# State scan of a hybrid diffusion block: clamped differences as relu on ScalarE, two multiplies on GpSimd

## The chip, the cores and the metric

One core of a Trainium2 chip runs the whole two-layer program in one launch. The metric is the device time of that launch in microseconds (us); lower is better. The engines are TensorE (PE; its weight loads are PEld), VectorE (DVE), ScalarE (ACT), GpSimd (POOL) and SyncE (SP).

## The reference

Two layers over 1024 latent and 256 context tokens. The second has a long convolution beside a bidirectional state-space scan. The change touches that scan alone, which per direction computes, for chunks of 128 tokens:

```python
acs = jnp.cumsum(adt, axis=-1)
decay_states = jnp.exp(acs[..., -1:] - acs)
states = jnp.einsum('bclgn,bgecl,bclgep->bcgepn', bc, decay_states, x)
...
wdiag = jnp.einsum('bclgn,bcsgn->bgcls', cc, bc)[:, :, None] * jnp.exp(segsum(adt))
y_diag = jnp.einsum('bgecls,bcsgep->bclgep', wdiag, x)
y_off = jnp.einsum('bclgn,bcgepn,bgecl->bclgep', cc, states[:, :-1], jnp.exp(acs))
```

There are 8 heads of 64 columns in 2 groups, state size 128, everything in fp32. segsum takes the differences of the running sums on the lower triangle. Context chunks come first and only carry the state on; latent chunks also give an output y.

## The kernel before, in words

`scan_states` works through 20 units (direction, chunk), the two directions in turn: `units`, of which u = 0 to 3 are context and give no output, and u = 4 to 19 are latent, with output number i = 0 to 15 (the dictionary `Y`). Each engine has its own program over the same units, in the order written, tied by semaphores.

Of one unit:

- GpSimd multiplies a triangle by the rates adt into adt_spread, [128, 8 heads, 128] (L1655, one unit ahead), and x by dt into x_dt (L1664, output units).
- TensorE makes the running sums of all heads along the free axis by a product of adt_spread with all ones (L1587, PSUM banks 0 and 1), and along the partitions by the triangle (L1588, bank 2). It makes them for unit u + 1 right after the state product of unit u (L1605), and ahead of the output products of unit u (L1619 with segments and x_dt, L1620 with the old state and exp_acs). The gram of an output unit (L1598) stands at its start, ahead of its state product.
- ScalarE copies the small sums to acs_source (L1633), takes the exponential of each head's total to decay_chunk (L1634) and, in output units, of all sums to exp_acs (L1639). It then takes the exponential of acs_left to decay_source (L1644) and that of the segments (L1647).
- VectorE takes total less sum to acs_left (L1684, reads PSUM), the differences of all sums to segments (L1689, reads PSUM, 1024 columns), multiplies decay_source by dt (L1691) and x by it to x_weighted (L1696), clamps the segments at zero (L1700), multiplies exp_acs by C (L1705), masks the gram (L1708), multiplies the segments by it (L1712), multiplies the old state by decay_chunk to state_kept (L1718), adds the state product (L1723), and reads the output of the unit before (L1569, or L1572 where it adds to the other direction's).

The state product needs x_weighted; the next running sums wait until all readers of the PSUM banks 0 to 2 are done (act_read, last_made, seg_made). Most tiles have two buffers; state_kept has one.

```python
HL = [P, H, CH]      # 128 x 8 x 128
HX = [P, H, HD]      # 128 x 8 x 64
acs_ps = g.ps[:, 0:2, :].rearrange("p b (h l) -> p (b h) l", l=CH)
by_head = lambda ap, shape: ap.unsqueeze(2).to_broadcast(shape)
```

Of the kernel before, what the change touches and what calls it, by code (L numbers as in the profile page):

```python
# [23 lines left out]
P = 128  # L24
# [1469 lines left out]
def scan_states(nc, g, d, xbc, gate, dt, adt, out):  # L1494
# [44 lines left out]
    names = ("spread sums acs_out act_read last_made seg_made decay_done clamped seg_exp decay_dt weighted x_dt c_scaled gram "  # L1539
             "masked attended state_product kept state y_product y_out cleared")  # L1540
    with stage(nc, names) as (mem, sems):
        (spread, sums, acs_out, act_read, last_made, seg_made, decay_done, clamped, seg_exp, decay_dt, weighted, x_dt,
# [14 lines left out]
        tmp = tile(nc, mem, "state_kept", [P, H, HD])  # L1557
# [4 lines left out]
        with nc.Block() as block:  # L1562
# [12 lines left out]
            def _(pe):  # L1575
                def running_sums(u):
# [3 lines left out]
                    if u >= 1:  # L1580

                        pe.wait_ge(act_read, u)
                        pe.wait_ge(last_made, u)
                        if ny(u):
                            pe.wait_ge(seg_made, ny(u))
# [38 lines left out]
            def _(act):  # L1624
                for u, (dr, c) in enumerate(units):
                    end = CH - 1 if dr == 0 else 0
                    act.wait_ge(sums, u + 1)
                    if u >= 2:
                        act.wait_ge(last_made, u - 1)
                        if ny(u - 1):  # L1630
                            act.wait_ge(seg_made, ny(u - 1))
                        act.wait_ge(kept, u - 1)
                    act.activation(acs[:, u % 2, :], g.ps[:, 2, 0:H], ACT.Copy).then_inc(acs_out, 1)  # L1633
                    done = act.activation(whole[:, u % 2, :], acs_ps[:, :, end], ACT.Exp)  # L1634
                    if u in Y:
                        i = Y[u]
                        if i >= 2:
                            act.wait_ge(y_product, i - 1)
                        done = act.activation(ea[:, i % 2], acs_ps, ACT.Exp)  # L1639
# [5 lines left out]
                    if u in Y:  # L1645
                        act.wait_ge(clamped, i + 1)
                        act.activation(seg[:, i % 2], seg[:, i % 2], ACT.Exp).then_inc(seg_exp, 1)  # L1647

            @block.gpsimd
            def _(pool):  # L1650
# [14 lines left out]

                spread_adt(0)
                for u, (dr, c) in enumerate(units):
                    if u + 1 < U:
                        spread_adt(u + 1)
                    if u in Y:  # L1670
# [3 lines left out]
            def _(dve):  # L1674
                dve.memset(st[:], 0.0).then_inc(cleared, 1)
                dve.wait_ge(cleared, 1)
                for u, (dr, c) in enumerate(units):
                    end = CH - 1 if dr == 0 else 0
                    tok = slice(c * CH, (c + 1) * CH)
                    dve.wait_ge(acs_out, u + 1)  # L1680
                    dve.wait_ge(act_read, u + 1)
                    if u >= 2:
                        dve.wait_ge(decay_done, u - 1)
                    dve.tensor_tensor(last[:, u % 2, :], acs_ps[:, :, end], acs[:, u % 2, :], ALU.subtract).then_inc(last_made, 1)  # L1684
                    if u in Y:
                        i = Y[u]
                        if i >= 2:
                            dve.wait_ge(y_product, i - 1)
                        dve.tensor_tensor(seg[:, i % 2], acs_ps, by_head(acs[:, u % 2, :], HL), ALU.subtract).then_inc(seg_made, 1)  # L1689
# [922 lines left out]
```

## Time and profile before

| what | value |
|---|---|
| median of 3 runs | 4232.28 us (4231.64 to 4232.49) |
| the profiled execution | 4226.73 us, span of its trace 4224.9 us |
| busy share of the span | PE 87%, PEld 64%, DVE 42%, ACT 30%, POOL 3% |
| instructions | 44523 |
| the scan (second stage of `scan_states`) | about 2636 to 2816 us of the span |

The span begins at the first instruction of the trace. Times in the rows below are microseconds from the start of the span unless marked ns; a busy share is over the whole program, of which the scan is about 4%. In a timeline a line gives start, length, engine, source line and operation, output<-inputs with their shape, the count of merged instructions, and in brackets the idle time ahead of it with what ended it. "psum" as the output of a matmul line is followed by its two operands. A length on DVE or POOL includes the time in which the engine was held up inside the instruction.

### The profile page before, as it was taken

The numbers are of one execution on the slowest core, as the hardware profiler recorded it, in microseconds if no ns is written. First come the engines' busy times: TensorE is split into PE (matmuls) and PEld (weight loads), VectorE is DVE, ScalarE is ACT, GpSimd is POOL, SyncE is SP. The second block draws the span as 40 slices with busy tenths as digits, with TensorE's granted clock in tenths as the row PEclk, the third lists the DMA queues.
The fourth block names the chain that finished last, engine by engine and source line by source line (L and its number), as shares of the span: only waits on it lengthen the run. The fifth ranks groups of instructions, "written<-read, shape, count | busy, mean of one in ns | idle before, by whom it ended". The sixth has DMA issues, their size and how long they took to land. (4 is left out here: it accounts for less than half of the span.)

```text
span 4224.9 us, 44523 instructions
## 1 busy us (share of the span) xinstructions
PE 3667.2 (87%) x17492; PEld 2713.8 (64%) x17492; DVE 1786.6 (42%) x2458; ACT 1258.7 (30%) x2138; POOL 134.6 (3%) x108
## 2 busy tenths in 40 slices
PE   6987788788895999999995999756898759999997
PEld 3663466566673888888883877432344538888885
DVE  2222556555407333333336432775255244333334
ACT  3322467666524111111114222220100232221122
POOL 0000000000001000000001000310000010000001
PEclk7998899999997999999998999875999979999998
DMA  7623310110003111111103210001320121111112
GB/s 292 252 93 101 92 26 14 50 35 17 25 17 124 40 36 38 40 37 37 40 25 119 90 50 22 1 34 60 123 84 25 60 94 51 46 49 50 50 45 94
DMA packets 98569, 272.31 MB, mean 64 GB/s; under 512 B 18205, under 2 KB 33053, under 8 KB 94276
## 3 DMA queue, kind: packets, MB, share of 16 engines
q1 hardware_dynamic: 98436, 270.51, 18.9%
q8 instruction: 86, 1.41, 0.1%
q14 instruction: 47, 0.39, 0.0%
HBM read 220.41 MB, written 50.07 MB: 64 GB/s over the span
## 5 line engine op out<-in xcount | busy, mean ns | idle before, releaser
L569 PE MATMUL psum<-h_high,w_high 128*128 128x512 f32 (+1 forms) x1280 | 472.7, 369 | 51.3 <-DVE w_low L648 51.3
L569 PE MATMUL psum<-h_low,w_high 128*128 128x512 f32 (+1 forms) x1280 | 472.3, 369 | 0.0
L569 PE MATMUL psum<-h_high,w_low 128*128 128x512 f32 (+1 forms) x1280 | 471.8, 369 | 0.0
L582 PE MATMUL psum<-hid_low,w_high 128*128 128x512 f32 (+1 forms) x1280 | 471.5, 368 | 0.0
L582 PE MATMUL psum<-hid_high,w_high 128*128 128x512 f32 (+1 forms) x1280 | 471.3, 368 | 0.0
L582 PE MATMUL psum<-hid_high,w_low 128*128 128x512 f32 (+1 forms) x1280 | 470.8, 368 | 0.0
L513 PE MATMUL psum<-h_high,w_high 128*128 128x512 f32 (+1 forms) x944 | 367.8, 390 | 37.3 <-DVE w_low L506 24.4
L645 DVE TENSOR_TENSOR out<-out,psum 128x512 f32<-128x512 f32 x320 | 202.7, 634 | 463.3 <-PE psum L582 463.3
L513 PE MATMUL psum<-h_high,w_low 128*128 128x512 f32 (+1 forms) x944 | 349.3, 370 | 0.0
L513 PE MATMUL psum<-h_low,w_high 128*128 128x512 f32 (+1 forms) x944 | 348.8, 370 | 0.0
L595 ACT ACTIVATE w_high<-w_raw 128x1024 fp32r<-128x1024 f32 x126 | 132.7, 1053 | 663.2 <-PE psum L582 662.8
L635 DVE TENSOR_TENSOR hid_high<-hid_relu 128x512 fp32r<-128x512 f32 x160 | 102.2, 639 | 477.9 <-ACT hid_relu L610 477.9
L569 PEld LDWEIGHTS psum<-h_high,w_high 128*128 128x128 f32 x1280 | 242.1, 189 | 93.2 <-DVE w_low L648 28.9
L1209 DVE TENSOR_REDUCE row_max<-psum 128x1 f32<-128x1280 f32 (+1 forms) x160 | 204.1, 1276 | 189.1 <-PE psum L1151 187.3
L1165 PE MATMUL psum<-identity,probs 128*128 128x128 f32 x1344 | 213.6, 287 | 65.0 <-ACT probs_turned L1240 35.1
L569 PEld LDWEIGHTS psum<-h_low,w_high 128*128 128x128 f32 x1280 | 242.2, 189 | 40.1
L569 PEld LDWEIGHTS psum<-h_high,w_low 128*128 128x128 f32 x1280 | 242.0, 189 | 40.5
L582 PEld LDWEIGHTS psum<-hid_high,w_high 128*128 128x128 f32 x1280 | 241.4, 189 | 40.8
L582 PEld LDWEIGHTS psum<-hid_high,w_low 128*128 128x128 f32 x1280 | 241.1, 188 | 40.4
L582 PEld LDWEIGHTS psum<-hid_low,w_high 128*128 128x128 f32 x1280 | 241.4, 189 | 39.9
L610 ACT ACTIVATE hid_relu<-psum 128x512 f32<-128x512 f32 x160 | 89.0, 556 | 559.8 <-PE psum L569 559.8
L513 PEld LDWEIGHTS psum<-h_high,w_high 128*128 128x128 f32 x944 | 178.9, 189 | 77.0 <-DVE w_low L506 23.6
(359 smaller groups left out, 5449.3 us busy)
## 6 DMA issues: line engine op xcount, KB each, us to landing
w_raw<-in_ff_w_dram SPq DMA_DIRECT2D x128, 512.0 KB
ada_ring<-in_ada_w_dram SPq DMA_DIRECT2D x24, 2048.0 KB, 8.7
scratch_x<-x SPq DMA_DIRECT2D x6, 2048.0 KB, 7.2
x<-scratch_x SPq DMA_DIRECT2D x6, 2048.0 KB
x<-in_x_dram SPq DMA_DIRECT2D x4, 2048.0 KB, 11.8
w_raw<-in_w_out_dram SPq DMA_DIRECT2D x16, 512.0 KB
scratch_spectra<-spectrum_out SPq DMA_DIRECT2D x32, 256.0 KB, 2.0
filter_ring<-scratch_spectra SPq DMA_DIRECT2D x16, 512.0 KB, 4.9
```

Of the source, the lines that this page charges most:

```text
L513: mm = pe.matmul(out, x[:, k, :], y[:, k, a:a + n], start=(k == 0 and i == 0), stop=(k == KT - 1 and i == 2))
L569: mm = pe.matmul(g.ps[:, u % BANKS, 0:n], x[:, k, :], y[:, k, a:a + n], start=(k == 0 and i == 0), stop=(k == KT - 1 and i == 2))
L582: mm = pe.matmul(g.ps[:, BANKS + u % BANKS, 0:n], x[:, k * 2 + half, :], y[:, k, a:a + n], start=(k == 0 and i == 0), stop=(k == HT - 1 an ...
L595: act.activation(w_hi[:, slot], raw[:, slot], ACT.Copy).then_inc(w_rounded, 1)
L610: act.activation(relu[:, u % 2, 0:n], g.ps[:, u % BANKS, 0:n], ACT.Relu).then_inc(up_free, 1)
L635: dve.tensor_tensor(hid_hi[:, j, a:a + n], relu[:, u % 2, 0:n], relu[:, u % 2, 0:n], ALU.mult).then_inc(rounded, 1)
L645: dve.tensor_tensor(out[:, m, a:a + n], out[:, m, a:a + n], g.ps[:, BANKS + u % BANKS, 0:n], ALU.add).then_inc(down_free, 1)
L1165: mm = pe.transpose(g.ps[:, 6 + r % 2, (kt - lo) * P:(kt - lo + 1) * P], p[:, x % 3, (kt - first) * P:(kt - first + 1) * P], g.ident[:])
L1209: dve.tensor_reduce(neg_max[:, x % 4:x % 4 + 1], flat, AX.X, ALU.max, negate=True).then_inc(maxed, 1)
```

## The change

The differences of the running sums are no longer taken and clamped on VectorE. ScalarE reads them from PSUM, one head at a time, as relu(acs - sums) with the head's column of acs_source as bias, and the later exponential takes a scale of -1. ScalarE also copies each head's total to a new tile acs_ends, so that acs_left reads only SBUF, and the running sums wait for ScalarE alone. x_weighted and state_kept are made on GpSimd, between the spread multiply and x_dt; state_kept gets a second buffer. VectorE's order of what is left is: acs_left, decay_source by dt, exp_acs by C, the gram's mask, segments by gram, state, output of the unit before.

```diff
--- before.py
+++ after.py
@@ -1536,10 +1536,10 @@
                     dst = xt[:, c, :] if kind == 0 else bt[:, c, :]
                     act.activation(dst, g.ps[:, i % 4, 0:dst.shape[1]], ACT.Copy).then_inc(read_out, 1)
 
-    names = ("spread sums acs_out act_read last_made seg_made decay_done clamped seg_exp decay_dt weighted x_dt c_scaled gram "
+    names = ("spread sums acs_out act_read last_made clamped decay_done seg_exp decay_dt weighted x_dt c_scaled gram "
              "masked attended state_product kept state y_product y_out cleared")
     with stage(nc, names) as (mem, sems):
-        (spread, sums, acs_out, act_read, last_made, seg_made, decay_done, clamped, seg_exp, decay_dt, weighted, x_dt,
+        (spread, sums, acs_out, act_read, last_made, clamped, decay_done, seg_exp, decay_dt, weighted, x_dt,
          c_scaled, gram, masked, attended, state_product, kept, state, y_product, y_out, cleared) = sems
         HL = [P, H, CH]
         HX = [P, H, HD]
@@ -1554,7 +1554,8 @@
         ea = tile(nc, mem, "exp_acs", [P, 2, H, CH])
         gm = tile(nc, mem, "gram_masked", [P, 2, G, CH])
         st = tile(nc, mem, "states", [P, 2, 2, H, HD])
-        tmp = tile(nc, mem, "state_kept", [P, H, HD])
+        tmp = tile(nc, mem, "state_kept", [P, 2, H, HD])
+        ends = tile(nc, mem, "acs_ends", [P, 2, H])
         y = out.y
         acs_ps = g.ps[:, 0:2, :].rearrange("p b (h l) -> p (b h) l", l=CH)
         by_head = lambda ap, shape: ap.unsqueeze(2).to_broadcast(shape)
@@ -1580,9 +1581,6 @@
                     if u >= 1:
 
                         pe.wait_ge(act_read, u)
-                        pe.wait_ge(last_made, u)
-                        if ny(u):
-                            pe.wait_ge(seg_made, ny(u))
                     for b in range(2):
                         pe.matmul(g.ps[:, b, :], g.ones[:], au[:, u % 2, 4 * b:4 * b + 4, :].rearrange("p h l -> p (h l)"), start=True, stop=True)
                     pe.matmul(g.ps[:, 2, 0:H], tri[:, dr, :], adt[:, c, 8 * dr:8 * dr + 8], start=True, stop=True).then_inc(sums, 1)
@@ -1627,15 +1625,17 @@
                     act.wait_ge(sums, u + 1)
                     if u >= 2:
                         act.wait_ge(last_made, u - 1)
-                        if ny(u - 1):
-                            act.wait_ge(seg_made, ny(u - 1))
                         act.wait_ge(kept, u - 1)
                     act.activation(acs[:, u % 2, :], g.ps[:, 2, 0:H], ACT.Copy).then_inc(acs_out, 1)
+                    act.activation(ends[:, u % 2, :], acs_ps[:, :, end], ACT.Copy).then_inc(acs_out, 1)
                     done = act.activation(whole[:, u % 2, :], acs_ps[:, :, end], ACT.Exp)
                     if u in Y:
                         i = Y[u]
                         if i >= 2:
                             act.wait_ge(y_product, i - 1)
+                        act.wait_ge(acs_out, 2 * u + 2)
+                        for h in range(H):
+                            act.activation(seg[:, i % 2, h, :], acs_ps[:, h, :], ACT.Relu, scale=-1.0, bias=acs[:, u % 2, h:h + 1]).then_inc(clamped, 1)
                         done = act.activation(ea[:, i % 2], acs_ps, ACT.Exp)
                     done.then_inc(act_read, 1)
                     act.wait_ge(last_made, u + 1)
@@ -1643,8 +1643,8 @@
                         act.wait_ge(weighted, u - 1)
                     act.activation(dec[:, u % 2, :], last[:, u % 2, :], ACT.Exp).then_inc(decay_done, 1)
                     if u in Y:
-                        act.wait_ge(clamped, i + 1)
-                        act.activation(seg[:, i % 2], seg[:, i % 2], ACT.Exp).then_inc(seg_exp, 1)
+                        act.wait_ge(clamped, H * (i + 1))
+                        act.activation(seg[:, i % 2], seg[:, i % 2], ACT.Exp, scale=-1.0).then_inc(seg_exp, 1)
 
             @block.gpsimd
             def _(pool):
@@ -1663,10 +1663,26 @@
                     xh = xt[:, c, :].rearrange("p (h x) -> p h x", x=HD)
                     pool.tensor_tensor(xd[:, i % 2], xh, by_head(dt[:, c, 8 * dr:8 * dr + 8], HX), ALU.mult).then_inc(x_dt, 1)
 
+                def x_by_decay(u):
+                    c = units[u][1]
+                    pool.wait_ge(decay_dt, u + 1)
+                    if u >= 2:
+                        pool.wait_ge(state_product, u - 1)
+                    xh = xt[:, c, :].rearrange("p (h x) -> p h x", x=HD)
+                    pool.tensor_tensor(xw[:, u % 2], xh, by_head(dec[:, u % 2, :], HX), ALU.mult).then_inc(weighted, 1)
+
+                def keep_state(u):
+                    pool.wait_ge(act_read, u + 1)
+                    pool.wait_ge(state, u - 1) if u >= 2 else pool.wait_ge(cleared, 1)
+                    old = st[:, units[u][0], (u // 2) % 2]
+                    pool.tensor_tensor(tmp[:, u % 2], old, by_head(whole[:, u % 2, :], HX), ALU.mult).then_inc(kept, 1)
+
                 spread_adt(0)
                 for u, (dr, c) in enumerate(units):
                     if u + 1 < U:
                         spread_adt(u + 1)
+                    x_by_decay(u)
+                    keep_state(u)
                     if u in Y:
                         x_by_dt(u)
 
@@ -1677,33 +1693,21 @@
                 for u, (dr, c) in enumerate(units):
                     end = CH - 1 if dr == 0 else 0
                     tok = slice(c * CH, (c + 1) * CH)
-                    dve.wait_ge(acs_out, u + 1)
-                    dve.wait_ge(act_read, u + 1)
+                    dve.wait_ge(acs_out, 2 * u + 2)
                     if u >= 2:
                         dve.wait_ge(decay_done, u - 1)
-                    dve.tensor_tensor(last[:, u % 2, :], acs_ps[:, :, end], acs[:, u % 2, :], ALU.subtract).then_inc(last_made, 1)
+                    dve.tensor_tensor(last[:, u % 2, :], ends[:, u % 2, :], acs[:, u % 2, :], ALU.subtract).then_inc(last_made, 1)
+                    dve.wait_ge(decay_done, u + 1)
+                    dve.tensor_tensor(dec[:, u % 2, :], dec[:, u % 2, :], dt[:, c, 8 * dr:8 * dr + 8], ALU.mult).then_inc(decay_dt, 1)
                     if u in Y:
                         i = Y[u]
-                        if i >= 2:
-                            dve.wait_ge(y_product, i - 1)
-                        dve.tensor_tensor(seg[:, i % 2], acs_ps, by_head(acs[:, u % 2, :], HL), ALU.subtract).then_inc(seg_made, 1)
-                    dve.wait_ge(decay_done, u + 1)
-                    dve.tensor_tensor(dec[:, u % 2, :], dec[:, u % 2, :], dt[:, c, 8 * dr:8 * dr + 8], ALU.mult).then_inc(decay_dt, 1)
-                    dve.wait_ge(decay_dt, u + 1)
-                    if u >= 2:
-                        dve.wait_ge(state_product, u - 1)
-                    xh = xt[:, c, :].rearrange("p (h x) -> p h x", x=HD)
-                    dve.tensor_tensor(xw[:, u % 2], xh, by_head(dec[:, u % 2, :], HX), ALU.mult).then_inc(weighted, 1)
-                    if u in Y:
-                        dve.wait_ge(seg_made, i + 1)
-
-                        dve.tensor_scalar(seg[:, i % 2], seg[:, i % 2], 0.0, None, ALU.min).then_inc(clamped, 1)
-                    if u in Y:
                         dve.wait_ge(act_read, u + 1)
                         grouped = [P, G, H // G, CH]
                         ea4 = ea[:, i % 2].rearrange("p (g e) l -> p g e l", g=G)
                         dve.tensor_tensor(ea4, ea4, by_head(xbc[:, 6:8, tok], grouped), ALU.mult).then_inc(c_scaled, 1)
                         dve.wait_ge(gram, i + 1)
+                        if i >= 2:
+                            dve.wait_ge(attended, i - 1)
                         g2 = g.ps[:, 4, 0:G * CH].rearrange("p (g l) -> p g l", g=G)
                         dve.tensor_tensor(gm[:, i % 2], g2, tri[:, dr, :].unsqueeze(1).to_broadcast([P, G, CH]), ALU.mult).then_inc(masked, 1)
                         dve.wait_ge(masked, i + 1)
@@ -1711,16 +1715,12 @@
                         s4 = seg[:, i % 2].rearrange("p (g e) l -> p g e l", g=G)
                         dve.tensor_tensor(s4, s4, by_head(gm[:, i % 2], grouped), ALU.mult).then_inc(attended, 1)
 
-                    dve.wait_ge(act_read, u + 1)
-                    if u >= 2:
-                        dve.wait_ge(state, u - 1)
-                    old, new = st[:, dr, (u // 2) % 2], st[:, dr, (u // 2 + 1) % 2]
-                    dve.tensor_tensor(tmp[:], old, by_head(whole[:, u % 2, :], HX), ALU.mult).then_inc(kept, 1)
+                    new = st[:, dr, (u // 2 + 1) % 2]
                     dve.wait_ge(kept, u + 1)
                     dve.wait_ge(state_product, u + 1)
                     if u - 2 in Y:
                         dve.wait_ge(y_product, Y[u - 2] + 1)
-                    dve.tensor_tensor(new, tmp[:], g.ps[:, 3, :].rearrange("p (h x) -> p h x", x=HD), ALU.add).then_inc(state, 1)
+                    dve.tensor_tensor(new, tmp[:, u % 2], g.ps[:, 3, :].rearrange("p (h x) -> p h x", x=HD), ALU.add).then_inc(state, 1)
                     if u in Y and i >= 1:
                         y_read(dve, i - 1)
                 y_read(dve, len(ys) - 1)
```

## Rows read from the trace of the kernel before

**Rows 1.** Windows: us; busy of PE, PEld, DVE, ACT, POOL; clock; DMA share, GB/s.

```profile
2674.30:2804.00 129.70, 95.83 (x659) 67.01 (x658) 119.32 (x161) 36.46 (x75) 42.69 (x29) 0.88 0.00 1
```

**Rows 2.** Timeline of TensorE: first and last running sums of the output units.

```profile
2674.05 0.28 PE L1588 MATMUL psum<-adt,triangles 128*128 128x8 f32 x2
...
2803.70 0.28 PE L1588 MATMUL psum<-adt,triangles 128*128 128x8 f32 x2
```

**Rows 3.** Timeline of TensorE, one unit of each kind.

```profile
2701.21 0.34 PE L1588 MATMUL psum<-adt,triangles 128*128 128x8 f32 x2
...
2705.43 1.13 PE L1605 MATMUL psum<-x_weighted,b_tokens 128*128 128x256 f32 x4 [1.29 <-DVE x_weighted L1696]
...
2714.39 1.54 PE L1605 MATMUL psum<-x_weighted,b_tokens 128*128 128x256 f32 x4 [2.97 <-DVE x_weighted L1696]
```

**Rows 4.** Windows over product and sums of four units.

```profile
2705.43:2708.39 2.96, 2.96 (x10) 1.81 (x10) 2.93 (x4) 1.06 (x1) 0.00 (x0) 1.00 0.00 0
2714.39:2719.05 4.66, 4.66 (x12) 2.62 (x14) 4.59 (x7) 1.06 (x1) 0.00 (x0) 0.63 0.01 4
2766.72:2771.08 4.36, 4.36 (x12) 2.75 (x13) 4.29 (x6) 1.06 (x1) 0.00 (x0) 0.67 0.00 0
2783.92:2789.63 5.71, 5.71 (x12) 3.23 (x13) 5.13 (x7) 1.06 (x1) 0.00 (x0) 0.50 0.01 3
```

**Rows 5.** Timeline of VectorE around one unit of the long kind.

```profile
2708.62 2.39 DVE L1718 TENSOR_TENSOR state_kept<-states,decay_chunk 128x512 f32<-128x512 f32 x1
...
2712.25 0.15 DVE L1684 TENSOR_TENSOR acs_left<-psum,acs_source 128x8 f32<-128x8 f32 x1
2712.32 1.21 DVE L1689 TENSOR_TENSOR segments<-psum,acs_source 128x1024 f32<-128x1024 f32 x1
...
2713.64 0.69 DVE L1696 TENSOR_TENSOR x_weighted<-x_tokens,decay_source 128x512 f32<-128x512 f32 x1
2714.25 0.69 DVE L1700 TENSOR_SCALAR segments<-segments 128x1024 f32<-128x1024 f32 x1
2714.85 1.22 DVE L1705 TENSOR_TENSOR exp_acs<-exp_acs,xbc 128x1024 f32<-128x1024 f32 x1
```

**Rows 6.** Timeline of GpSimd in the same stretch.

```profile
2708.48 1.98 POOL L1655 TENSOR_TENSOR adt_spread<-triangles,adt 128x1024 f32<-128x1024 f32 x1 [3.85 <-PE psum L1588]
...
2710.86 1.05 POOL L1664 TENSOR_TENSOR x_dt<-x_tokens,dt 128x512 f32<-128x512 f32 x1 [0.40 <-PE psum L1620]
...
2719.13 1.90 POOL L1655 TENSOR_TENSOR adt_spread<-triangles,adt 128x1024 f32<-128x1024 f32 x1 [7.22 <-PE psum L1588]
```

**Rows 7.** Timeline of VectorE in the fourth unit, without output.

```profile
2667.25 1.49 DVE L1696 TENSOR_TENSOR x_weighted<-x_tokens,decay_source 128x512 f32<-128x512 f32 x1
```

**Rows 8.** Timeline of ScalarE: elsewhere, and in the long unit.

```profile
334.09 0.45 ACT L915 ACTIVATE v_tile<-psum 128x128 f32<-128x128 f32 x2 [2.14 <-PE psum L872]
...
1320.99 1.93 ACT L414 ACTIVATE h_high<-norm_scaled,modulation 128x512 fp32r<-128x512 f32 x3
...
2708.43 0.18 ACT L1633 ACTIVATE acs_source<-psum 128x8 f32<-128x8 f32 x1 [1.37 <-PE psum L1588]
...
2708.57 1.03 ACT L1639 ACTIVATE exp_acs<-psum 128x1024 f32<-128x1024 f32 x1
...
2712.44 0.21 ACT L1644 ACTIVATE decay_source<-acs_left 128x8 f32<-128x8 f32 x1 [2.84 <-DVE acs_left L1684]
```

**Rows 9.** Groups by shape, ScalarE: count, busy us, mean ns, idle.

```profile
L1240 ACT ACTIVATE probs_turned<-psum 128x256 f32<-128x256 f32 x160 | 61.5, 384 | 13.7 <-PE psum L1165 9.9
...
L1265 ACT ACTIVATE probs<-psum,row_max 128x256 f32<-128x256 f32 x32 | 15.1, 473 | 0.0
...
L414 ACT ACTIVATE h_high<-norm_scaled,modulation 128x512 fp32r<-128x512 f32 x48 | 33.5, 718 | 22.4 <-DVE norm_scaled L466 22.4
...
L915 ACT ACTIVATE v_tile<-psum 128x128 f32<-128x128 f32 x10 | 2.6, 277 | 18.0 <-DMA scratch_v_a<-v_tile 15.9 <-PE psum L872 2.1
...
L1634 ACT ACT_TABLE_LOAD x1 | 1.3, 1283 | 0.0
```
## The prediction

> **What bounds the stage now.** The change touches only the state scan, so I read that stage from coarse to fine. The window [rows 1] over the sixteen units with output (four without come first) is 129.7 us, in which VectorE is busy 119.32 us, TensorE 95.83, GpSimd 42.69 and ScalarE only 36.46. A change that takes work from DVE looks right by that row. But this share is an average over two kinds of unit. From the last of the running sums of the first unit with output to that of the last unit [rows 2] lie 15 periods in 2803.98 - 2674.33 = 129.65 us, 8.64 us each. The TensorE timeline [rows 3] shows what they consist of: a state product, two all-ones products and the small sums (call their end T), then the output products, the gram, and an idle wait for x_weighted. In one kind the sums end at 2701.55 and the product starts at 2705.43, in the other they end at 2708.39, the end of the first window of [rows 4], and it starts at 2714.39: waits of 3.88 and 6.00 us from T. The 6.00 leave TensorE 2.97 us idle just before the product, and behind it the same ten matmuls take 4.66 us instead of 2.96. The windows over product and sums [rows 4] give the reason: granted clock 1.00 in the first, 0.67 and 0.50 in others, which is 2.4 GHz against a part or all of the stretch at 1.2 GHz. Of the 15 stretches eight take 2.96 and seven take 4.36 to 5.71, and each of these seven stands behind an idle wait of about 3 us, none of the eight behind more than 1.3. So the kernel alternates a long period (6.00 + 4.66 = 10.66) and a short one (3.88 + 2.96 = 6.84). The loop is T, ScalarE, DVE, TensorE, T; the state products and the next running sums are in it, the output products aren't.
>
> Why is one long? In DVE's timeline [rows 5] state_kept takes 2.39 us instead of the 0.69 of an equal multiply, since it runs against the 1.98 us spread multiply of GpSimd [rows 6]. So acs_left starts only at 2712.25, 3.86 behind T, and then come the large subtraction with the small multiply behind it (1.32 from the one's start to the start of x_weighted) and x_weighted (0.69).
>
> **What the change removes.** From DVE: 16 subtractions (1.1 start to start: the 1.32 less some 0.2 for the small multiply), 16 clamps (0.60), 20 x_weighted (0.61) and 20 state_kept (0.69) [rows 5]: about 3.0 us per output unit, plus the held-up time of the last. Nothing of DVE's old backlog then stands ahead of acs_left. In the four first units there is also a gain: x_weighted took 1.49 in one of them [rows 7], held by GpSimd, and the small multiply ahead of it was held likewise. Summed over the four, the waits T to product shrink by 0, 0.7, 0.7 and 1.5 us, as the spread multiply now comes earlier in GpSimd's order, while the 512-element multiply itself is 1.05 there [rows 6] against 0.69. I take **-3 us** for these four.
>
> **What it adds to the loop.** I build one output unit from T.
> - ScalarE starts 0.04 behind T, at 2708.43 [rows 4, 8]. acs and ends start 0.07 apart, ends is written by 0.28, and the new wait on acs_out lets the first relu go at 0.32.
> - Eight relus of 128x128 out of PSUM with a bias column. None exists in the trace. Without a bias column the 128x128 copy lasts 0.277 [rows 9], and two, start to end, take 0.45 [rows 8], so 0.17 apart. The column adds 473 - 384 = 89 ns to a 256-wide one, hence 0.26. From the other side, three 512-wide ones with a column take 1.93 us [rows 8]; at 0.718 each [rows 9] that is 0.606 apart; less 384 columns at (384 - 277)/128 = 0.84 ns, 0.28. Bounds: 0.17 (the column is free when pipelined) and 0.37 (0.277 + 0.089, no overlap). I take 0.28, the nearest row with a column: 8 x 0.28 = 2.24, so exp_acs starts at 2.56.
> - exp_acs (1.03 [rows 8]) and the exponential of acs_left behind it: 0.21 long, done 1.14 behind the start of exp_acs, at 3.70. In this order the decay stands behind nine large reads that it doesn't need. The segment exponential comes after it and is no part of the loop.
> - DVE: small multiply at 3.74. Its next instruction, exp_acs times C, needs nothing more and starts 0.08 later, as the next one does today [rows 5]. It reads two SBUF tiles for 1.1 us, until 4.92.
> - GpSimd's x_weighted can only ask once the small multiply has ended, at about 3.95 (3.74 and the 0.15 that acs_left takes for as many columns, and a hop), so it comes second. That such a pair excludes each other is what state_kept's 2.39 shows, and the other way round GpSimd's 1.98 against its usual 1.90 [rows 6]: it waits for the last 0.09 of DVE's segments multiply. It runs 4.92 to 5.96. Bounds of this hold-up: 0 and 1.1 us; I take 0.95.
> - Product at 6.02, so TensorE waits from T **6.02 us**, as in the long kind (6.00).
>
> Beside the loop: GpSimd then does state_kept, x_dt and the next spread (1.05 + 1.05 + 1.90), done some 2.2 behind the next T; 5.0 of the period. acs_left, which now reads two SBUF tiles, may be held until then, and is needed only at 3.5: hidden, with 1.3 to spare. If relus were at 0.17 that cover would be 0.4. DVE's segments multiply is held behind x_weighted to 7.1, x_dt ends at 9.2; the output products need both and start about 0.2 behind the next T. They and the gram take 2.7 at full clock (today from some 0.3 behind T until 2714.39 - 2.97 = 2711.42 [rows 3]), so TensorE idles 6.02 - 0.2 - 2.7 = 3.1 us ahead of each product. The extra read ends costs 0.07 in each unit and is in the sum. The added waits of the relus (y_product of two units back) are long met. The tail behind the last sums I put at nothing: the same steps, 12 us in both.
>
> **The clock is the other term.** A wait of 2.97 was followed by 4.36, 4.66 or 5.71 for product and sums [rows 3, 4], and now every unit has one. I take 4.4, the lowest, as one unit in a regular row of such gaps may be touched less than wholly; bounds 2.96 (no fall) and 5.71. Period 6.0 + 4.4 = 10.4. Sum: 15 x (10.4 - 8.64) = +26.4, less 3 = **+23 us**. The profiled execution took 4226.73 (span 4224.9), 5.55 below the median 4232.28 of the runs; I put the difference on the median: 4255.
>
> Two rules of the Trainium skill bear on this. The page "ScalarE: Activation LUTs" (Rules for kernel authors) says to use VectorE and not ScalarE for relu; its figures (What ACT_TABLE_LOAD costs) of 280 ns + 0.833 ns per element with a pointer bias, less an overlap of 93, give 0.294 per relu, an estimate by which the total would be 1.7 us higher, 4257. The page "SBUF — State Buffer" (Who interferes with whom) says that a DVE instruction with two SBUF inputs and a GpSimd one that reads SBUF exclude each other and that the order of issue decides who blocks. The rows of state_kept and of the spread agree, and by it the port-free rival below falls.
>
> **Rivals.**
> - *The port doesn't bite* (not slower): GpSimd gets x_weighted in ahead of DVE's exp_acs multiply. Then product at 5.08, TensorE's gap 2.1 us, between the 1.3 that keeps the clock and the 2.97 that loses it. Kept: period 8.04, -3 - 9 = -12, **4220**; lost: 9.5, 4242. For it: DVE has only 4.2 us of work left. Against: DVE's multiply has no wait left to give way. It decides if x_weighted starts below 4.2 us behind T. 0.16 (0.12 faster, 0.04 within).
> - *The clock falls seldom*: period 9.0 to 9.8, -3 + 5 to 17: **4235 to 4247**. The seven of seven speak against, but those gaps came every second unit. 0.19 (0.06 within).
> - *Longer still*: relus at 0.37, or stretches near 5.71: period 11.1 to 11.7, **4266 to 4275**. 0.16.
> - *Table switch*: were Relu and Exp not in one table, two loads of 1.28 us would stand in every unit, +41 us, near 4296. The trace has one load for Copy and Exp at L1634 [rows 9]. The ScalarE page (Table sets: the hidden batching unit) says relu is in every set, against it. 0.03.
> - *No effect*: DVE's relief and ScalarE's load cancel, 4232. 0.04.
>
> The forecast, every period like today's long one, has 0.42 and spans 4248 to 4265. A measurement of this kernel can tell about 0.2%, 8.5 us. Slower: 0.42 + 0.16 + 0.13 + 0.03 = 0.74; within: 0.06 + 0.04 + 0.04 = 0.14; faster 0.12. The range leaves out the port-free case, no effect and the table switch: 4236 to 4278.
>
> **What would show it.** The changed profile should have: relus 0.28 apart; decay_source's exponential about 3.5 behind T; exp_acs times C starting ahead of x_weighted, which shows as late or long on GpSimd; TensorE idle about 3 us ahead of each of the 16 output units' products; granted clock of the stage near 0.75, down from 0.88; DVE busy well below 119 us without a shorter stage. Relus at 0.17 apart, or a stage at clock 1.00, would prove it wrong.

## The result and the profile after

The changed kernel takes 4254.41 us, the median of 4 runs (4254.13 to 4254.73), against 4231.96 for the kernel before in the same comparison (4228.3 to 4232.49). The ratio is 1.0058, with a 95% interval of 1.0046 to 1.0070: slower, by 22.4 us in the medians. In the profiled executions the spans are 4252.6 and 4224.9, 27.7 apart; the profiled execution of before was some 5 us faster than its median. The scan alone accounts for 21.7 of the 27.7, as shown below.

The page of the changed kernel, span and part 1:

```profile
span 4252.6 us, 44639 instructions
...
PE 3681.4 (87%) x17492; PEld 2720.9 (64%) x17492; DVE 1723.5 (41%) x2386; ACT 1292.0 (30%) x2286; POOL 204.0 (5%) x148
```

DVE fell from 42% to 41% of the span and GpSimd rose from 134.6 us busy to 204.0, as the diff says. Neither sets the stage. The window over the 15 periods of the output units, the columns as in [rows 1]:

```profile
2669.03:2823.85 154.82, 103.92 (x661) 73.56 (x661) 69.95 (x104) 66.69 (x210) 100.05 (x59) 0.82 0.00 1
```

154.82 us for 15 periods is 10.32 each, against 8.64. VectorE is busy 69.95 us in place of 119.32, TensorE's granted clock is 0.82 in place of 0.88. The engine that the old window named as fullest was relieved by more than a third, and the stage became longer. The TensorE timeline, with the first and the last sums of output units as in [rows 2], the same kinds of line as in [rows 3] between them, and behind it the window over that unit's product and sums, as in [rows 4]:

```profile
2668.75 0.30 PE L1586 MATMUL psum<-adt,triangles 128*128 128x8 f32 x2
...
2710.82 0.28 PE L1586 MATMUL psum<-adt,triangles 128*128 128x8 f32 x2
...
2717.01 2.07 PE L1603 MATMUL psum<-x_weighted,b_tokens 128*128 128x256 f32 x4 [3.31 <-POOL x_weighted L1672]
...
2823.57 0.28 PE L1586 MATMUL psum<-adt,triangles 128*128 128x8 f32 x2
```

```profile
2717.01:2721.42 4.41, 4.41 (x12) 2.79 (x13) 2.31 (x3) 0.00 (x0) 4.41 (x3) 0.66 0.01 4
```

From the end of the sums (T = 2710.82 + 0.28 = 2711.10) to the product are 5.91 us, 3.31 of them idle just before it, and product and sums take 4.41 at a clock of 0.66. Before, every second unit was like this; now all are. The short kind, 6.84, is gone. Over the 15 periods of either trace the waits from T to the product add up to 87.8 us in place of 71.7, and product and sums to 67.0 in place of 58.0: some 16 us of the loss are waiting, some 9 are slower products. The last twelve periods are 10.24 to 10.34.

What fills the 5.91 us stands in the timelines of the three other engines over that unit. ScalarE's:

```profile
2711.15 0.18 ACT L1629 ACTIVATE acs_source<-psum 128x8 f32<-128x8 f32 x1 [5.87 <-PE psum L1586]
...
2711.48 2.23 ACT L1638 ACTIVATE segments<-psum,acs_source 128x128 f32<-128x128 f32 x8
2713.56 1.06 ACT L1639 ACTIVATE exp_acs<-psum 128x1024 f32<-128x1024 f32 x1
2714.46 0.26 ACT L1644 ACTIVATE decay_source<-acs_left 128x8 f32<-128x8 f32 x1
```

VectorE's:

```profile
2711.42 0.17 DVE L1699 TENSOR_TENSOR acs_left<-acs_ends,acs_source 128x8 f32<-128x8 f32 x1 [1.35 <-ACT acs_ends L1630]
2714.75 0.17 DVE L1701 TENSOR_TENSOR decay_source<-decay_source,dt 128x8 f32<-128x8 f32 x1 [3.16 <-ACT decay_source L1644]
2714.84 1.22 DVE L1707 TENSOR_TENSOR exp_acs<-exp_acs,xbc 128x1024 f32<-128x1024 f32 x1
...
2716.43 1.61 DVE L1716 TENSOR_TENSOR segments<-segments,gram_masked 128x1024 f32<-128x1024 f32 x1
```

And GpSimd's, from the spread multiply made ahead for the next unit to x_dt:

```profile
2709.51 1.89 POOL L1655 TENSOR_TENSOR adt_spread<-triangles,adt 128x1024 f32<-128x1024 f32 x1
2715.00 1.96 POOL L1672 TENSOR_TENSOR x_weighted<-x_tokens,decay_source 128x512 f32<-128x512 f32 x1 [3.60 <-DVE decay_source L1701]
2716.92 2.02 POOL L1678 TENSOR_TENSOR state_kept<-states,decay_chunk 128x512 f32<-128x512 f32 x1
2718.90 1.04 POOL L1664 TENSOR_TENSOR x_dt<-x_tokens,dt 128x512 f32<-128x512 f32 x1
```

Read them in the order of the chain. The eight relus start at 2711.48 and exp_acs at 2713.56, so 2.08 us for eight, 0.26 each. acs_left was ready at 2711.59, but its exponential stands behind them and ends at 2714.72, 3.62 behind T. VectorE multiplies it at 2714.75 and starts exp_acs times C 0.09 later. GpSimd has its semaphore at 2715.00, and its x_weighted lasts 1.96, of which 1.04 would be its own work: it ends at 2716.96, as late as if it had begun at 2715.92. The product follows at 2717.01. A recorded start on GpSimd isn't the start of the work: the hold-up lies inside the length. The same shows in the other direction: VectorE's multiply of the segments takes 1.61 where its like of 1024 columns takes 1.22, and GpSimd's state_kept behind it 2.02.

Two of the waits of the stage (us in total, times, longest):

```profile
POOL x_weighted L1672 <- DVE decay_source L1701: 74.2, 20, 5.6
...
PE psum L1603 <- POOL x_weighted L1672: 63.7, 20, 5.2
```

TensorE waits for x_weighted 20 times, 63.7 us; GpSimd itself had idled 74.2 us until the small multiply let it begin. So GpSimd's own time isn't what is lacking, though TensorE's line alone would read so.

### The profile page after: what moved, and what is told of

Same layout as the page of the kernel before. It is cut to its first block and busy times, and to the rows that moved or that the text cites. A ratio compares the mean times of both kernels' runs of the same rounds, so it can differ in the third digit from the quotient of the medians.

```text
span 4252.6 us, 44639 instructions
## 1 busy us (share of the span) xinstructions
PE 3681.4 (87%) x17492; PEld 2720.9 (64%) x17492; DVE 1723.5 (41%) x2386; ACT 1292.0 (30%) x2286; POOL 204.0 (5%) x148
```

## The experiments

The theory: three terms make the loss, in a row. (a) ScalarE's order puts eight relus and exp_acs ahead of the decay. (b) VectorE's exp_acs multiply then holds the port ahead of x_weighted; "the port" stands here for whatever makes two such instructions of VectorE and GpSimd run one behind the other, the later one with its hold-up inside its length. (c) The idle time that this leaves TensorE costs it its clock. The rivals: the relus as such are too dear on ScalarE; the two multiplies as such are too slow on GpSimd; a shared port is full in any order. Nine kernels ran, the first four beside one set of runs of the kernel before, then three, then two. Times are medians, ratios are to the kernel before; "wait" is from T to the product, "P+S" product and sums, both in a steady unit; a period that is not marked as a mean is that of a steady unit.

| kernel | us | ratio (95% interval) | wait | P+S | period |
|---|---|---|---|---|---|
| before | 4232 | 1 | 6.00 / 3.88 | 4.66 / 2.96 | 8.64 mean |
| changed | 4254.4 | 1.0058 (1.0046 to 1.0070) | 5.91 | 4.41 | 10.32 mean |
| e3_clock_kept | 4235.2 | 1.0009 (0.9999 to 1.0019) | 5.90 | 2.97 | 8.81 |
| e2_port_free | 4221.2 | 0.9974 (0.9961 to 0.9987) | 4.94 | 2.96 | 7.90 |
| e1_decay_first | 4233.7 | 1.0000 (0.9990 to 1.0010) | 5.4 | 3.9 | 9.31 |
| e4_relu_only | 4223.8 | 0.9978 (0.9968 to 0.9988) | 4.54 | 2.96 / 4.60 | 7.5 / 9.1 |
| e5_gpsimd_only | 4209.3 | 0.9954 (0.9937 to 0.9971) | 4.39 | 2.96 | 7.35 |
| e6_first_and_psum | 4207.8 | 0.9948 (0.9932 to 0.9965) | 3.6 to 6.1 | 2.9 to 3.5 | 6.6 to 9.0 |
| e7_all_three | 4234.1 | 1.0008 (0.9998 to 1.0017) | 2.8 / 5.6 | 3.4 / 6.15 | 6.2 / 11.7 |
| e8_between | 4210.1 | 0.9952 (0.9935 to 0.9969) | 4.44 | 2.96 | 7.40 |
| e9_between_dve | 4217.1 | 0.9965 (0.9951 to 0.9980) | 4.21 | 2.97 | 7.18 |

### The clock by itself

```diff
                         mm.then_inc(gram, 1)
+                        for _ in range(3):
+                            pe.matmul(g.ps[:, 7, :], g.ones[:], xt[:, c, :], start=True, stop=True)
```

> The changed kernel with work added: three 128x512 products into a PSUM bank that nobody reads stand behind each gram, about 2.6 us at 2.4 GHz, which fills most of TensorE's idle 3.26 us. Theory (the clock is a term of its own): product and sums take 2.96 instead of 4.35 us, the wait stays 5.85, the period is about 8.9 and the whole about 4233, though more matmuls run. Rival (product and sums are long for another reason, or the idle time doesn't set the clock): 4254 or more.

Measured 4235.22, period 8.81. In its TensorE timeline the filler stands at L1599 and the wait is as long as in the changed kernel (2712.21 less 2706.03 + 0.28, 5.90), but what follows is short:

```profile
2706.03 0.28 PE L1586 MATMUL psum<-adt,triangles 128*128 128x8 f32 x2
...
2708.99 2.74 PE L1599 MATMUL psum<-x_tokens,all_ones 128*128 128x512 f32 x6
2712.21 1.13 PE L1605 MATMUL psum<-x_weighted,b_tokens 128*128 128x256 f32 x4 [0.48 <-POOL x_weighted L1674]
```

```profile
2712.21:2715.18 2.97, 2.97 (x10) 1.82 (x10) 2.04 (x3) 0.00 (x0) 2.97 (x3) 1.00 0.00 0
```

Granted clock 1.00 and 2.97 us, in place of 0.66 and 4.41. More work on TensorE, on no one's behalf, takes 19 us off the time. By count the changed kernel loses 15 x 1.4 = 21 us to the clock. That isn't the whole of its loss against the kernel before, which lost some 14 us to it itself (58.0 less 15 x 2.96): e3 gets back what both lose, and is then no slower than the kernel before in spite of the longer waits. And the clock is the effect, not the cause: it takes the idle time to lose it.

### The hold-up at the port by itself

```diff
                         dve.wait_ge(act_read, u + 1)
+                        dve.wait_ge(weighted, u + 1)
```

> The changed kernel with one wait more: VectorE's exp_acs multiply waits until x_weighted is done, so that GpSimd always has the port first. Theory: x_weighted lasts 1.05 instead of 1.96, the product starts 4.9 us behind the sums' end instead of 5.85, and TensorE idles 2.3 us instead of 3.26. If the clock falls all the same the period is 9.3 and the whole 4239; if 2.3 us of idle keep it up, 7.9 to 8.5 and 4218 to 4227. Rival (the hold-up is hidden, another wait ends last): within 3 us of 4254.

Measured 4221.2, 33 us below the changed kernel and 0.26% below the one before, by one wait more. GpSimd's timeline, and then TensorE's:

```profile
2709.50 1.04 POOL L1672 TENSOR_TENSOR x_weighted<-x_tokens,decay_source 128x512 f32<-128x512 f32 x1 [1.09 <-DVE decay_source L1701]
...
2711.50 2.02 POOL L1664 TENSOR_TENSOR x_dt<-x_tokens,dt 128x512 f32<-128x512 f32 x1
```

```profile
2705.34 0.28 PE L1586 MATMUL psum<-adt,triangles 128*128 128x8 f32 x2
2706.71 0.45 PE L1617 MATMUL psum<-segments,x_dt 128*64 128x128 f32 x4 [1.09 <-DVE segments L1717]
...
2710.60 1.13 PE L1603 MATMUL psum<-x_weighted,b_tokens 128*128 128x256 f32 x4 [1.23 <-POOL x_weighted L1672]
```

x_weighted is down to 1.04, and the wait to 2710.60 - 2705.62 = 4.98, as forecast (4.9). The idle time just before the product isn't 2.3 but 1.23. VectorE, which has waited, ends its multiply of the segments only at 2706.65, so the output products idle 1.09 behind the sums and end closer to the next product (x_dt, held for 2.02 by the exp_acs multiply, is ready before that). So the better branch came true, for a reason that I had not seen: the idle time was split in two, besides being shortened. TensorE does wait for VectorE here, but the loop from T to the product doesn't.

### ScalarE's order

```diff
                     act.activation(ends[:, u % 2, :], acs_ps[:, :, end], ACT.Copy).then_inc(acs_out, 1)
+                    act.wait_ge(last_made, u + 1)
+                    if u >= 2:
+                        act.wait_ge(weighted, u - 1)
+                    act.activation(dec[:, u % 2, :], last[:, u % 2, :], ACT.Exp).then_inc(decay_done, 1)
                     done = act.activation(whole[:, u % 2, :], acs_ps[:, :, end], ACT.Exp)
...
                     done.then_inc(act_read, 1)
-                    act.wait_ge(last_made, u + 1)
-                    if u >= 2:
-                        act.wait_ge(weighted, u - 1)
-                    act.activation(dec[:, u % 2, :], last[:, u % 2, :], ACT.Exp).then_inc(decay_done, 1)
```

> The changed kernel with one move: ScalarE makes decay_source's exponential ahead of decay_chunk, the relus and exp_acs. Theory (the loop is ScalarE's nine large reads, then a multiply held by VectorE): the decay leaves the reads behind, x_weighted starts within about 2.3 us of the sums' end and meets no exp_acs multiply, the idle time of TensorE ahead of the product falls below 1.5 us, its clock stays up, the period falls from 10.3 to 7.5 - 8.0 us, and the whole to 4207 - 4225. Rival (GpSimd is too slow or the shared port is full, wherever the decay stands): the period stays above 9.5 and the whole above 4242.

Measured 4233.65, period 9.31: better than the changed kernel by 21 us, but neither theory's number. ScalarE's timeline shows a wait that I had left out:

```profile
2701.94 0.17 ACT L1630 ACTIVATE acs_ends<-psum 128x8 f32<-128x8 f32 x1
2705.66 0.21 ACT L1634 ACTIVATE decay_source<-acs_left 128x8 f32<-128x8 f32 x1 [3.55 <-DVE acs_left L1699]
...
2705.84 2.17 ACT L1642 ACTIVATE segments<-psum,acs_source 128x128 f32<-128x128 f32 x8
```

VectorE's line of that acs_left, and then GpSimd's in the same stretch:

```profile
2703.97 1.66 DVE L1699 TENSOR_TENSOR acs_left<-acs_ends,acs_source 128x8 f32<-128x8 f32 x1
```

```profile
2699.69 2.08 POOL L1678 TENSOR_TENSOR state_kept<-states,decay_chunk 128x512 f32<-128x512 f32 x1 [1.80 <-ACT exp_acs L1643]
2701.73 2.02 POOL L1664 TENSOR_TENSOR x_dt<-x_tokens,dt 128x512 f32<-128x512 f32 x1
2703.71 1.89 POOL L1655 TENSOR_TENSOR adt_spread<-triangles,adt 128x1024 f32<-128x1024 f32 x1
```

ScalarE idles 3.55 us for acs_left, for two reasons. The sums end at T = 2701.83, but VectorE comes to acs_left only at 2703.97, since the rest of the unit before stands ahead of it in VectorE's order. And then it is held: acs_left is eight columns, but since the change it reads two SBUF tiles, and it came behind the spread multiply that GpSimd had begun at 2703.71 (1.66 long). The relus, now behind the decay, wait with it, and the next sums wait for exp_acs behind the relus (0.68 idle ahead of them; the clock is 1.00 in this stretch). In the changed kernel itself there is no such hold: acs_left takes 0.17 in all 20 units, asking at 2711.42 when the spread multiply has ended at 2711.40. To test the hold, e6 gives acs_left its PSUM operand back:

```diff
-                    dve.tensor_tensor(last[:, u % 2, :], ends[:, u % 2, :], acs[:, u % 2, :], ALU.subtract).then_inc(last_made, 1)
+                    dve.tensor_tensor(last[:, u % 2, :], acs_ps[:, :, end], acs[:, u % 2, :], ALU.subtract).then_inc(last_made, 1)
```

> As e1_decay_first, with acs_left read from PSUM as in the kernel before (no acs_ends; the running sums wait for last_made again). Theory on e1's miss: its acs_left, reading two SBUF tiles, stood behind GpSimd's x_dt and spread multiply until 3.8 us behind the sums' end, and ScalarE's relus behind it. Without that hold the relus start 0.9 behind the sums' end, only the small multiply and x_weighted wait for the spread (product at about 5.1), and the period falls from 9.31 to about 8.0: 4212 to 4222. Rival (e1 is limited by the sum of port time, in any order): period above 9, 4229 or more.

Measured 4207.75, the lowest median, though e5 and e8 lie within the noise of it; periods of 6.6, 7.8 and 9.0 with a mean of 7.74, against a mean of 8.96 in e1. acs_left now passes in 0.15 us, and the small multiply behind it takes the hold (1.23), where it hurts less. ScalarE still idles 1.96 us for acs_left in one of the 7.8 periods, which is VectorE's own part. Better than forecast by 4 us, and the rival is out.

The gentler form moves the decay only between the relus and exp_acs:

```diff
                             act.activation(seg[:, i % 2, h, :], acs_ps[:, h, :], ACT.Relu, scale=-1.0, bias=acs[:, u % 2, h:h + 1]).then_inc(clamped, 1)
+                        act.wait_ge(last_made, u + 1)
+                        if u >= 2:
+                            act.wait_ge(weighted, u - 1)
+                        act.activation(dec[:, u % 2, :], last[:, u % 2, :], ACT.Exp).then_inc(decay_done, 1)
                         done = act.activation(ea[:, i % 2], acs_ps, ACT.Exp)
...
```

> The changed kernel with one move: ScalarE makes decay_source's exponential between the eight relus and exp_acs. Theory: it comes 0.9 us sooner, and VectorE's exp_acs multiply can't stand ahead of x_weighted any more, since exp_acs isn't there yet: product about 4.2 us behind the sums' end instead of 5.85, TensorE's idle time near 1 us, clock up, and GpSimd's 5.0 us with what the port adds (7.35 in e5_gpsimd_only) becomes the bound: period 7.3 to 7.8, 4207 to 4215. Rival (the decay must stand ahead of the relus to help): 4225 or more.

Measured 4210.13, period 7.40. GpSimd over one period:

```profile
2706.57 1.89 POOL L1660 TENSOR_TENSOR adt_spread<-triangles,adt 128x1024 f32<-128x1024 f32 x1
2709.00 1.04 POOL L1677 TENSOR_TENSOR x_weighted<-x_tokens,decay_source 128x512 f32<-128x512 f32 x1 [0.55 <-DVE decay_source L1706]
2710.00 2.02 POOL L1683 TENSOR_TENSOR state_kept<-states,decay_chunk 128x512 f32<-128x512 f32 x1
2711.99 2.02 POOL L1669 TENSOR_TENSOR x_dt<-x_tokens,dt 128x512 f32<-128x512 f32 x1
```

VectorE's acs_left of the same unit:

```profile
2706.82 1.66 DVE L1704 TENSOR_TENSOR acs_left<-acs_ends,acs_source 128x8 f32<-128x8 f32 x1
```

x_weighted is 1.04, as exp_acs times C can't be ahead of it, and GpSimd has 0.55 idle in 7.40. The rest is 1.89 + 1.04 + 2.02 + 2.02 less small overlaps, the two long ones held by one VectorE multiply each. The 0.55 hang on GpSimd as well: acs_left is held behind the spread multiply until 2708.48, and the decay, the small multiply and x_weighted follow one behind the other. So GpSimd with what it holds up is now the bound. Whether acs_left from PSUM, as in e6, would gain more in this order was not run. This version keeps every part of the change and beats both kernels; the relus needn't be behind the decay, exp_acs does.

### The two halves of the change, each alone

e4 is the changed kernel with the two multiplies at VectorE again:

```diff
+                    dve.tensor_tensor(xw[:, u % 2], xh, by_head(dec[:, u % 2, :], HX), ALU.mult).then_inc(weighted, 1)
...
+                    dve.tensor_tensor(tmp[:, u % 2], old, by_head(whole[:, u % 2, :], HX), ALU.mult).then_inc(kept, 1)
...
-                    x_by_decay(u)
-                    keep_state(u)
```

> The changed kernel with x_weighted and state_kept back on VectorE, at the places that they had; relus, acs_ends and ScalarE's order as changed. Theory: the decay still waits for the nine reads (3.3 us behind the sums' end), but x_weighted follows at once with 0.69 us, so the product starts at about 4.5, TensorE idles about 1.9 us, and the period is 7.5 (clock up) to 8.9 (clock down): 4215 to 4236. Rival (the relus on ScalarE are the whole loss): 4245 or more.

Measured 4223.79. The relus aren't the loss: with them alone (and what comes with them, acs_ends and the second buffer of state_kept) the kernel gains 0.22%. Two neighbouring products in its TensorE timeline, and the windows over product and sums behind each:

```profile
2713.37 1.13 PE L1603 MATMUL psum<-x_weighted,b_tokens 128*128 128x256 f32 x4 [2.00 <-DVE x_weighted L1704]
...
2720.88 1.13 PE L1603 MATMUL psum<-x_weighted,b_tokens 128*128 128x256 f32 x4 [1.95 <-DVE x_weighted L1704]
```

```profile
2713.37:2716.33 2.96, 2.96 (x12) 1.88 (x13) 2.93 (x4) 0.00 (x0) 0.00 (x0) 1.00 0.02 6
2720.88:2725.48 4.60, 4.60 (x12) 2.47 (x14) 4.53 (x6) 0.00 (x0) 0.00 (x0) 0.63 0.00 0
```

Idle times of 2.00 and 1.95, and yet 2.96 us at clock 1.00 after the one and 4.60 at 0.63 after the other. The length of the idle time before a product doesn't decide by itself.

e5 is the other half: the kernel before, with the multiplies at GpSimd.

```diff
+                    x_by_decay(u)
+                    keep_state(u)
...
-                    dve.tensor_tensor(xw[:, u % 2], xh, by_head(dec[:, u % 2, :], HX), ALU.mult).then_inc(weighted, 1)
...
-                    dve.tensor_tensor(tmp[:], old, by_head(whole[:, u % 2, :], HX), ALU.mult).then_inc(kept, 1)
```

> The kernel before with x_weighted and state_kept moved to GpSimd and the second state_kept buffer, nothing else: differences and clamp stay on VectorE. Theory: x_weighted is held by the clamp (0.6 us) only, the product starts about 4.3 us behind the sums' end, but GpSimd's 5.0 us and VectorE's 3 us of two-input or clamp work share a port, so that the period is 8.0 to 8.8: 4222 to 4235. Rival (GpSimd's moves are the whole loss): 4245 or more.

Measured 4209.28, 0.46% below the kernel before and 13 us below the lower end of what I expected. Its GpSimd timeline, one period:

```profile
2707.95 1.89 POOL L1655 TENSOR_TENSOR adt_spread<-triangles,adt 128x1024 f32<-128x1024 f32 x1
2709.95 1.42 POOL L1672 TENSOR_TENSOR x_weighted<-x_tokens,decay_source 128x512 f32<-128x512 f32 x1
2711.33 2.02 POOL L1678 TENSOR_TENSOR state_kept<-states,decay_chunk 128x512 f32<-128x512 f32 x1
2713.32 2.02 POOL L1664 TENSOR_TENSOR x_dt<-x_tokens,dt 128x512 f32<-128x512 f32 x1
```

And VectorE's, between the small multiply and the exp_acs multiply:

```profile
2709.55 0.32 DVE L1707 TENSOR_TENSOR decay_source<-decay_source,dt 128x8 f32<-128x8 f32 x1
2709.79 0.68 DVE L1711 TENSOR_SCALAR segments<-segments 128x1024 f32<-128x1024 f32 x1
2710.39 2.06 DVE L1716 TENSOR_TENSOR exp_acs<-exp_acs,xbc 128x1024 f32<-128x1024 f32 x1
```

1.89 + 1.42 + 2.02 + 2.02 = 7.35, the period, without a gap: GpSimd is the bound, three of its multiplies held once each, by 0.4, 1.0 and 1.0. I had added VectorE's 3 us in full to GpSimd's 5.0; only 2.35 of them hold it. So each half alone gains (9 and 20 us), and together they lose 22. The relus put 2.1 us ahead of the decay. They also take the clamp out of VectorE's order, so that the exp_acs multiply stands right behind the small multiply and gets the port just when GpSimd needs it (exp_acs itself is finished before the decay in e5 too). With x_weighted at VectorE (e4) this doesn't matter, and in e5 only the clamp holds x_weighted, 0.4 us, while the exp_acs multiply comes second (2.06). Both halves have the second buffer of state_kept; what it is worth by itself was not run.

### Two that try for more

e7 joins the relus with the decay first, acs_left from PSUM and both multiplies at VectorE (the edits of e1, e6 and e4 together).

> Relus on ScalarE as changed, decay first, acs_left from PSUM, x_weighted and state_kept on VectorE: port time is 1.9 + 1.0 on GpSimd and some 3.7 on VectorE. Theory: the product starts about 2.9 us behind the sums' end, the next running sums at 4.1 when exp_acs has been read, and the period is 6.1 to 7.0, near TensorE's own 5.7 us at 2.4 GHz: 4192 to 4208. Rival (shared port time bounds it): 7.4 or more, 4213 or more.

Measured 4234.13: a miss, the rival's side by far. The sum of the port time says 6.6 us, but the periods alternate, 6.2 and 11.7. VectorE's line of state_kept in one such unit, and GpSimd's beside it:

```profile
2722.85 2.38 DVE L1725 TENSOR_TENSOR state_kept<-states,decay_chunk 128x512 f32<-128x512 f32 x1
```

```profile
2722.34 2.35 POOL L1655 TENSOR_TENSOR adt_spread<-triangles,adt 128x1024 f32<-128x1024 f32 x1 [2.69 <-PE psum L1587]
```

state_kept runs 2.38 against the spread multiply, as in [rows 5, 6], and everything behind it in VectorE's order is late; TensorE's clock falls in the next stretch (0.71 over the 5.94 us of product and sums from 2727.85). It is the old kernel's alternation again, with a larger swing. e9 puts only x_weighted at VectorE, on top of e8:

```diff
+                    dve.tensor_tensor(xw[:, u % 2], xh, by_head(dec[:, u % 2, :], HX), ALU.mult).then_inc(weighted, 1)
...
-                    x_by_decay(u)
```

> As e8_between, with x_weighted back on VectorE and state_kept left on GpSimd. Theory: GpSimd's own work falls from 5.0 to 4.0 us and is no longer the bound, product about 3.7 behind the sums' end, period 6.7 to 7.2: 4198 to 4206. Rival (as in e7_all_three: with x_weighted early, GpSimd's spread multiply falls on VectorE's work again and the periods alternate): 4215 or more.

Measured 4217.13, a miss, with the time in the rival's range (4215 or more) but not by the rival's mechanism: the periods don't alternate. The steady period is 7.18, at the upper end of the forecast. What undid it are the first four periods, 35.9 us together in place of 27.3 in e8. VectorE's x_weighted in one of them, and GpSimd's line beside it:

```profile
2662.40 2.34 DVE L1710 TENSOR_TENSOR x_weighted<-x_tokens,decay_source 128x512 f32<-128x512 f32 x1
```

```profile
2662.30 1.90 POOL L1660 TENSOR_TENSOR adt_spread<-triangles,adt 128x1024 f32<-128x1024 f32 x1
```

With no x_weighted in GpSimd's program, state_kept and the spread multiply start as soon as the sums are there and hold VectorE's x_weighted (2.34 in place of 0.69). An instruction that has left a queue no longer keeps back those behind it.

## Why the prediction was right

The forecast was 4255, measured 4254.41. By its own steps:

- **The first four units, -3.** From the first all-ones product of the stage to T of the first output unit: 2669.03 - 2636.10 = 32.93 after, 2674.33 - 2637.93 = 36.40 before; -3.5. The waits shrink by 2.8 of it, as forecast.
- **Relus, 0.28 each.** 0.26. The end of the estimate taken from a 256-wide pair of rows (0.26) was the better one; the estimate of 0.294 from the Trainium skill's figures (page "ScalarE: Activation LUTs", What ACT_TABLE_LOAD costs) is 13% high here. The rule of the same page (Rules for kernel authors) to keep relu on VectorE is not borne out in this kernel: e4, with the relus on ScalarE, is faster by 0.22%.
- **The decay at 3.70, the small multiply at 3.74, exp_acs multiply 0.08 behind.** 3.62, 3.65 and 0.09.
- **x_weighted second at the port, 4.92 to 5.96.** It ended at 5.86; held for 0.92 by its length, forecast 0.95. e2 shows that it is on the path: taken away, the wait falls by 0.93. The Trainium skill's page "SBUF — State Buffer" (Who interferes with whom) gives the rule, and the held lines here with two SBUF operands agree with it: whoever asks first goes first. In e5 the clamp too, which reads one SBUF tile, held GpSimd for 0.38.
- **The wait, 6.02; idle time 3.1; product and sums, 4.4.** 5.91; 3.3; 4.41, and e3 shows that the last is the clock. I took the lowest of the long stretches, and that is what a steady row of such units gives; the first had 5.02. The choice was in part luck: no row showed such a steady row, and with 4.66, the commonest long stretch of before, the sum would be 4 us higher.
- **The sum.** 15 x (10.32 - 8.64) = 25.2, less 3.5, is 21.7; the medians differ by 22.4. One sign was off: the granted clock of the stage was forecast near 0.75 and is 0.82.
- **Hidden hold of acs_left.** In the sum it is nothing, and that held. But I had GpSimd busy until 2.2 behind T by a period of 9.0, while forecasting 10.4; by the latter it ends some 0.7 behind T, and it ended 0.3 behind. So no hold came about at all, and none had to be hidden. e1, where acs_left is held, shows what the hold costs.
- **The port-free rival** was worked out at 4220 with the clock kept; e2, which enforces it, gives 4221.2, but with a gap of 1.2 and not 2.1. So the close number is in part luck; whether a steady gap of 2.1 keeps the clock is not shown.

What the prediction didn't see is the split. It read GpSimd's multiplies as a burden and the relus as the price; each alone gains, and I had e5 too slow by at least 13 us, since I added VectorE's port time to GpSimd's in full.

## What to carry to other kernels

Ask of each engine's order not how much stands in it but what stands ahead of the one small result that the loop waits for; moving one exponential ahead of one large read turned +0.58% into -0.48%. When work moves to GpSimd, look for the VectorE instruction with two SBUF inputs that is ready a moment sooner, and let it wait, or give it something that isn't ready. Test the halves of a change apart: two gains can make a loss, and the busy time of VectorE in the stage, down by more than a third here, says nothing of it.

## What was new about the hardware

- TensorE's clock: idle times of 1.95 to 2.0 us before the product in e4 are followed by 2.96 us (clock 1.00) or by 4.60 (0.63). In the kernel before it never fell behind an idle time of 1.3, in the changed one it always did behind 3.2 and more; between these it did either in e4. Even a longer idle time doesn't decide by itself: in e8 the first output unit idles 3.41 ahead of its product at 2673.51, and product and sums still take 2.97 at clock 1.00. In e6, with 0.17 idle ahead of most products, four of the fifteen periods still have a slow gram (up to 1.23 against 0.71): there the idle time, 2.03, lies ahead of the output products. What exactly the chip weighs these runs don't settle.
- Filling idle time with useless products (e3) gave back 19 us of 4254.
- The port between VectorE and GpSimd goes by who asks first, also over several instructions: in e1 acs_left, asking 0.26 us after the spread multiply had begun, was held for 1.5 us for a work of 0.15, while segments, asking during state_kept, ran between state_kept and x_dt, which had to wait in turn (2.02).
